# Tile 0's products with the high weights of two panels, done during tile 1's norm at two joints

## The reference

```python
def layer_norm(x, g, b):
    mu = jnp.mean(xf, axis=-1, keepdims=True)
    var = jnp.mean(jnp.square(xf - mu), axis=-1, keepdims=True)
    y = (xf - mu) * lax.rsqrt(var + LN_EPS)
    return y * g + b

def post_norm(x, sub, g, b):
    return layer_norm(DN_ALPHA * x + sub, g, b)

def swiglu(x, w1, w3, w2):
    return (jax.nn.silu(x @ w1) * (x @ w3)) @ w2
```

## Time and profile before

| | us |
|---|---|
| median of 3 runs | 2235.81 (2235.27 to 2235.83) |
| span of the profiled execution, first to last instruction | 2233.5 |
| the profiled execution's own time | not shown; the median is 2.3 above its span |
| TensorE busy | 2197.0 (98%) |
| VectorE busy | 1568.6 (70%) |
| ScalarE busy | 1170.0 (52%) |
| TensorE's granted clock, mean | 0.999 |

### The profile page before, as it was taken

One profiled execution on the slowest core, in us unless ns is written; L12 is line 12 of the kernel. 1 busy time (PEld: TensorE's weight loads), 2 busy tenths in 40 slices (PEclk: granted clock), 3 DMA queues, 4 the chain that ended last, 5 costly groups with the idle time before them and its releaser, 6 DMA issues. The chain is left out here.

```text
span 2233.5 us, 37259 instructions
## 1 busy us (share of the span) xinstructions
PE 2197.0 (98%) x14678; PEld 1964.0 (88%) x14678; DVE 1568.6 (70%) x2935; ACT 1170.0 (52%) x2008; POOL 33.9 (2%) x20
## 2 busy tenths in 40 slices
PE   8999999999999999999999999999999999999998
PEld 8987889999999998888888889988889788888887
DVE  7975659999889976666666557766657465776655
ACT  6643454555554455565555455545544544585544
POOL 0100000010000000000000000000000000000000
PEclk9999999999999999999999999999999999999999
DMA  7418425555444456666655556536455655404552
GB/s 275 151 46 189 170 93 174 181 178 170 144 150 143 150 171 192 194 194 193 194 189 212 190 190 240 191 127 232 176 200 191 248 186 192 175 34 175 184 204 97
DMA packets 78310, 389.98 MB, mean 175 GB/s; under 512 B 9771, under 2 KB 12715, under 8 KB 49868
## 3 DMA queue, kind: packets, MB, share of 16 engines
q1 hardware_dynamic: 76684, 383.33, 49.3%
q0 software_dynamic: 1040, 4.19, 1.5%
q10 hardware_dynamic: 432, 0.33, 0.0%
HBM read 382.57 MB, written 5.24 MB: 174 GB/s over the span
## 5 line engine op out<-in xcount | busy, mean ns | idle before, releaser
L256 DVE TENSOR_TENSOR split_slots<-ring,split_slots 128x1024 fp32r<-128x1024 f32 x402 | 475.3, 1227 | 118.4 <-ACT split_slots L247 118.2
L247 ACT ACTIVATE split_slots<-ring 128x1024 fp32r<-128x1024 f32 x402 | 402.3, 1054 | 149.3 <-PE banks L400 123.3
L3107 PE MATMUL banks<-x_transposed,split_slots 128*128 128x512 f32 x1360 | 478.4, 395 | 0.3 <-PEq L464 0.3
L409 DVE SCALAR_TENSOR_TENSOR expert_lo<-ring,expert_hi 128x512 fp32r<-128x512 f32 x512 | 353.4, 697 | 165.7 <-ACT expert_hi L404 164.6
L404 ACT ACTIVATE expert_hi<-ring 128x512 fp32r<-128x512 f32 x512 | 324.0, 634 | 252.5 <-PE banks L400 252.5
L3108 PE MATMUL banks<-x_transposed,split_slots 128*128 128x256 f32 x1360 | 381.5, 281 | 0.0
L3107 PEld LDWEIGHTS banks<-x_transposed,split_slots 128*128 128x128 f32 x1360 | 255.3, 188 | 60.4 <-issue 0.5
L398 PE MATMUL banks<-x_transposed,expert_hi 128*128 128x256 f32 x1024 | 293.9, 287 | 2.5 <-DVE expert_lo L409 2.5
L399 PE MATMUL banks<-x_transposed,expert_hi 128*128 128x256 f32 x1024 | 287.8, 281 | 0.0
L400 PE MATMUL banks<-x_transposed,expert_lo 128*128 128x256 f32 x1024 | 287.7, 281 | 0.0
L3108 PEld LDWEIGHTS banks<-x_transposed,split_slots 128*128 128x128 f32 x1360 | 256.4, 189 | 1.5
(11 more groups left out here) (491 smaller groups left out, 4020.5 us busy)
## 6 DMA issues: line engine op xcount, KB each, us to landing
ring<-in_ffn_w SPq DMA_DIRECT2D x132, 1024.0 KB, 4.8
ring<-in_peer_u SPq DMA_DIRECT2D x128, 512.0 KB, 3.5
ring<-in_peer_v SPq DMA_DIRECT2D x128, 512.0 KB, 3.6
ring<-in_w_in SPq DMA_DIRECT2D x16, 1024.0 KB, 6.0
ring<-in_sgu_w_in SPq DMA_DIRECT2D x16, 1024.0 KB, 4.8
ring<-in_peer_wq SPq DMA_DIRECT2D x8, 1024.0 KB, 7.3
ring<-in_sgu_w_out SPq DMA_DIRECT2D x8, 1024.0 KB, 4.9
ring<-in_kv_w SPq DMA_DIRECT2D x6, 1024.0 KB, 4.8
```

The source lines that it names most:

```text
L247: act.activation(self.parts[:, b, 0, p], self.k.w.slot(g)[:, p], ACT.Copy).then_inc(self.high_done, 1)
L256: ins = dve.tensor_tensor(self.parts[:, b, 1, p], self.k.w.slot(g)[:, p], self.parts[:, b, 0, p].bitcast(F32), ALU.subtract)
L409: return dve.scalar_tensor_tensor(dst, src, scale, hi.bitcast(F32), ALU.mult, ALU.subtract)
L3107: pe.matmul(out(j, slice(0, 2 * SEQ)), lh, k.xT.both[:, c, :, :], start=(c == 0), stop=False)
```

## The change

`SecondHigh` lets ScalarE write the high parts of the next stage's second panel during the norm. `TileAhead` then gives TensorE, between the transposes of tile 0 and those of tile 1, the products of both panels' high weights with tile 0: 16 per panel, each with the high and the low part of 128 rows as one operand (two runs of 128 columns), written to two runs of 128 columns of the output bank. The sums are started by products with a tile of zeros that clear the whole bank (`clear`). Behind the joint each panel then has 16 products of its low weights (256 columns) and 16 of the high weights with tile 1 (256 columns). It replaces the stand-ins at norms 1 and 4.

For that VectorE's order is changed. In all six norms: tile 1's first half is added ahead of tile 0's normalising. At norms 1 and 4 also: tile 0's two low parts are written behind tile 1's centring, ahead of its normalising. The first unit's sums lie in banks 0, 1 and 4, 5, the second's in 6, 7 and 4, 5. The diff, cut:

```diff
@@ -225,6 +225,8 @@
         self.beginning = k.beginning
+        self.second = k.second if self.begun else None
+        self.highs_begun = 2 if self.second else self.begun
         self.before = k.before
@@ -234,7 +236,7 @@
     def high(self, act, n, i=0, per=0):
-        if n < self.begun:
+        if n < self.highs_begun:
             return
@@ -252,7 +254,11 @@
             p = slice(half * SLOT // 2, (half + 1) * SLOT // 2)
-            dve.wait_ge(self.high_done, 2 * (n - self.begun) + half + 1 + 2 * per * i)
+            if n < self.highs_begun:
+                if self.before:
+                    dve.wait_ge(self.second.high_done, half + 1)
+            else:
+                dve.wait_ge(self.high_done, 2 * (n - self.highs_begun) + half + 1 + 2 * per * i)
             ins = dve.tensor_tensor(self.parts[:, b, 1, p], self.k.w.slot(g)[:, p], self.parts[:, b, 0, p].bitcast(F32),
...
@@ -309,10 +315,82 @@
+class SecondHigh:
+    def __init__(self, k, first):
+        self.k, self.g = k, first.g + 1
+        self.b = self.g % BUFFERS
+        self.high_done = k.sig.new()
+        k.second = self
+    def highs(self, act):
+        k = self.k
+        act.wait_ge(k.w.loaded[self.g % RING], 16 * (self.g // RING + 1))
+        for half in range(2):
+            p = slice(half * SLOT // 2, (half + 1) * SLOT // 2)
+            act.activation(k.split_parts[:, self.b, 0, p], k.w.slot(self.g)[:, p], ACT.Copy).then_inc(self.high_done, 1)
+class TileAhead:
+    def __init__(self, k, first, second):
+        self.k, self.first, self.second = k, first, second
+    def product(self, pe, begun, bank, j, c, i):
+        k = self.k
+        wh = k.split_parts[:, begun.b, 0, :].rearrange("p (c n) -> p c n", c=DC)
+        own = slice(i * P, (i + 1) * P)
+        out = k.psum[:, bank + j, :].rearrange("p (q n) -> p q n", q=2)[:, :, own]
+        return pe.matmul(out, wh[:, c, j * P:(j + 1) * P], k.xT.both[:, c, :, own], start=False,
+                         stop=(i == 1 and c == DC - 1))
+    def clear(self, pe, bank):
+        k = self.k
+        for j in range(2):
+            pe.matmul(k.psum[:, bank + j, :], k.zero[:, :], k.split_parts[:, self.first.b, 0, 0:2 * SEQ], start=True, stop=False)
+    def tile_0(self, pe, written):
+        g = self.first.g
+        pe.wait_ge(self.k.w.used[g % RING], g // RING + 1)
+        self.clear(pe, 0)
+        for part in range(2):
+            pe.wait_ge(written, part + 1)
+            for j in range(2):
+                for c in range(part * DC // 2, (part + 1) * DC // 2):
+                    self.product(pe, self.first, 0, j, c, 0)
+        pe.wait_ge(self.second.high_done, 2)
+        self.clear(pe, 4)
+        for j in range(2):
+            for c in range(DC):
+                self.product(pe, self.second, 4, j, c, 0)
+    def low_weights(self, pe, begun, bank, chunks):
+        k = self.k
+        wl = k.split_parts[:, begun.b, 1, :].rearrange("p (c n) -> p c n", c=DC)
+        for j in range(2):
+            for c in chunks:
+                pe.matmul(k.psum[:, bank + j, 0:SEQ], wl[:, c, j * P:(j + 1) * P], k.xT.hi[:, c, :], start=False, stop=False)
+    def tile_1(self, pe, begun, bank):
+        for j in range(2):
+            for c in range(DC):
+                ins = self.product(pe, begun, bank, j, c, 1)
+        return ins
 class Before:
...
-    def __init__(self, splits_eaten, highed=None, written=None, banks_read=(), parts=None, turn=None, ahead=0):
+    def __init__(self, splits_eaten, highed=None, written=None, banks_read=(), parts=None, turn=None, ahead=0,
+                 begun=None):
+        self.begun = begun
         self.splits_eaten, self.highed, self.written, self.banks_read = splits_eaten, highed, written, banks_read
...
@@ -431,6 +510,7 @@
         self.eps = self.sb(ctx, "epsilons", [P, 2])
+        self.zero = self.sb(ctx, "zeros", [P, P], F32R)
         self.final_stat = self.sb(ctx, "final_stats", [P, 4, TILES])
@@ -599,6 +679,8 @@
         act.activation(warm[:, :], k.eps[:, 0:1], ACT.Sqrt)
+        act.wait_ge(begun.ident_landed, 16)
+        act.activation(k.zero[:, :], k.ident[:, :], ACT.Copy, scale=0.0)
         for i in range(TILES):
@@ -2686,7 +2768,8 @@
-    def __init__(self, k, ctx, split, gains, which, slots, final=False, squares=None, last=False):
+    def __init__(self, k, ctx, split, gains, which, slots, final=False, squares=None, last=False,
+                 two_ahead=False):
         self.last = last
...
@@ -2726,26 +2810,25 @@
         dve.wait_ge(self.gains_landed, 32)
-        for i in range(TILES):
-            x = k.x[:, i, :]
-            sums = [stat[:, 6 * n, i:i + 1] for n in range(2)]
-            mean = stat[:, 1, i:i + 1]
-            def add(n):
-                own = x[:, self.halves[n]]
-                dve.wait_ge(self.tile_done, 2 * i + n + 1)
-                dve.scalar_tensor_tensor(own, own, DN_ALPHA, k.psum[:, 2 * i + n, :], ALU.mult, ALU.add, accum_out=sums[n]
-                                         ).then_inc(self.summed, 1)
-            add(0)
-            dve.wait_ge(self.summed, 2 * i + 1)
-            dve.tensor_scalar(mean, sums[0], -1.0 / D, None, ALU.mult).then_inc(self.negated, 1)
-            add(1)
-            dve.wait_ge(self.summed, 2 * i + 2)
-            dve.wait_ge(self.negated, 2 * i + 1)
-            dve.scalar_tensor_tensor(mean, sums[1], -1.0 / D, mean, ALU.mult, ALU.add).then_inc(self.negated, 1)
+        def add(i, n):
+            own, mean = k.x[:, i, self.halves[n]], stat[:, 1, i:i + 1]
+            dve.wait_ge(self.tile_done, 2 * i + n + 1)
+            dve.scalar_tensor_tensor(own, own, DN_ALPHA, k.psum[:, 2 * i + n, :], ALU.mult, ALU.add,
+                                     accum_out=stat[:, 6 * n, i:i + 1]).then_inc(self.summed, 1)
+            dve.wait_ge(self.summed, 2 * i + n + 1)
+            if n == 0:
+                dve.tensor_scalar(mean, stat[:, 0, i:i + 1], -1.0 / D, None, ALU.mult).then_inc(self.negated, 1)
+            else:
+                dve.wait_ge(self.negated, 2 * i + 1)
+                dve.scalar_tensor_tensor(mean, stat[:, 6, i:i + 1], -1.0 / D, mean, ALU.mult, ALU.add).then_inc(self.negated, 1)
+        def centre(i):
             dve.wait_ge(self.negated, 2 * i + 2)
-            dve.scalar_tensor_tensor(accumulated(k, i), x, stat[:, 1, i:i + 1], gains[:, 0, :], ALU.add, ALU.mult
+            dve.scalar_tensor_tensor(accumulated(k, i), k.x[:, i, :], stat[:, 1, i:i + 1], gains[:, 0, :], ALU.add, ALU.mult
                                      ).then_inc(self.gained, 1)
+        def normalise(i):
             dve.wait_ge(self.rooted, i + 1)
@@ -2753,8 +2836,19 @@
                                          ALU.mult, ALU.add).then_inc(self.normed, 1)
+        add(0, 0)
+        add(0, 1)
+        centre(0)
+        add(1, 0)
+        normalise(0)
+        add(1, 1)
+        centre(1)
+        if self.ahead:
+            self.low(dve, 0)
+            self.low(dve, 1)
+        normalise(1)
         if self.begin:
-            for b in range(4):
+            for b in range(2 if self.ahead else 0, 4):
                 self.low(dve, b)
@@ -2765,6 +2859,9 @@
             if self.begin and i == 1:
+                if self.ahead:
+                    self.split.finished(act, self.free + 1)
+                    self.ahead.second.highs(act)
                 self.high(act, 0)
@@ -2780,8 +2877,9 @@
         self.k.before = Before((self.tile_done, 2 * TILES), (self.highed, 4), (self.written, 4), ((self.written, 1),),
-                               turn=self.turn_last)
+                               turn=self.turn_last, begun=self.ahead)
         self.k.gains_free = self.normed
+        self.k.ahead = self.ahead
@@ -2790,17 +2888,19 @@
             stand_in(pe, self.k, 3)
-            if self.which != 0:
+            if self.ahead:
+                self.ahead.tile_0(pe, self.written)
+            elif self.which != 0:
                 pe.wait_ge(self.negated, 2 * TILES)
...
                 self.turn_last(pe, range(DC))
-                stand_in(pe, self.k, 8)
-def last_products(pe, k, tile_done, ready, operands, rows):
+                stand_in(pe, self.k, 8, 3)
+def last_products(pe, k, tile_done, ready, operands, rows, eaten=None):
@@ -2810,7 +2910,8 @@
         for half in range(2):
-            part(0, i, r, half)
+            ins = part(0, i, r, half)
+        return ins
@@ -2824,7 +2925,9 @@
     late(0)
-    early(1, 1)
+    ins = early(1, 1)
+    if eaten:
+        ins.then_inc(eaten, 1)
     late(1)
...
@@ -2876,7 +2979,7 @@
             last_products(pe, k, norm.tile_done, ready, lambda n, r: k.xT.at(slice(0, P), 2 * (last + n) + r),
-                          lambda n: split.rows(last + n))
+                          lambda n: split.rows(last + n), split.eaten)
             norm.tensor(pe)
@@ -3058,6 +3161,7 @@
         copied, joined = ([k.sig.new() for _ in range(2)] for _ in range(2))
+        ahead = k.ahead
```

(39 more changed lines are left out.)

## The result

| | median us | lowest to highest | runs |
|---|---|---|---|
| kernel before | 2235.82 | 2235.01 to 2237.80 | 20 |
| changed kernel | 2238.76 | 2237.53 to 2241.58 | 20 |

The account below looks back on a forecast made before the run. TensorE, busy for 98% of the span, was taken as the bound. Late joint 0.0, early joint 0.0, stall 0.2 and norms 2.1 summed to +2.3 us: span 2235.8, time 2238.1, range 2233 to 2242.

Parts of the forecast that it names:

- Late joint: Joint at about 2036 us: 3.8 us saved behind tile 1's transposes, 3.8 lost ahead of them, net 0.0.
- T: Start of tile 1's transposes on TensorE, 2041.03 us at the late joint, 1500.44 at the early; forecast 3.8 later at each.
- Early joint: Joint at about 1500 us, followed by a barrier: 3.8 us saved, tile 1's transposes 3.8 later, net 0.0.
- stall of 0.2: Early joint, fourth panel: TensorE may wait for VectorE's join of the second panel's sums; 0.2 us, bounds nothing and 1.0.
- sign of being wrong: At the fourth panel, a wait of over 0.5 us would show the prediction wrong.
- the near end: Fourth panel's wait: 0.2 us taken between bounds of nothing and 1.0, near the end that the sum itself gives.
- Plain norms: Three other norms that begin a next panel: VectorE's new order makes each 0.63 us late, together 1.9.
- the last norm: Norm without high parts on ScalarE: only the shift of the mean stays, 0.24 us.
- The 2.3 added to the span: Difference between the median, 2235.81 us, and the profiled span, 2233.5, carried over to the forecast time.
- Hidden: Rival, both joints: tile 0's products end before tile 1 is ready, transposes +1.0 instead of +3.8, time 2232.5 us; 10%.
- Clock: Rival, hole before tile 1's transposes: clock falls to 1.2 GHz, work there about 3.4 us longer per joint, 2244.9 us; 7%.
- Split output: Rival, tile products writing two runs of 128 columns take 0.234 us each, not 0.119; time 2253 us; 6%.

Follow-up runs that it names:

- e3: Changed kernel with the fourth panel's transfer issued ahead of the gains' and biases' transfers at both joints; 2237.66 us, ratio 1.0007 to the kernel before.
- e8: Kernel before with 14 stand-ins in place of 8 ahead of the barrier at 1164 us; 2236.23 us, ratio 0.9998 to the kernel before.
- e1: Changed kernel with VectorE's old order in the four norms that do nothing ahead; 2236.87 us, ratio 1.0003 to the kernel before.
- e6: Changed kernel with 8 more stand-ins at each joint, between tile 0's products and tile 1's transposes; 2242.87 us, ratio 1.0029 to the kernel before.
- e9: e7 with the second panel's products with tile 0 moved behind tile 1's transposes at the early joint, replacing 8 stand-ins; 2232.28 us, ratio 0.9981.
- e7: e5 with 14 stand-ins in place of 8 ahead of the barrier at 1164 us; 2232.79 us, ratio 0.9983 to the kernel before.
- e4: Changed kernel with tile 0 normalised before adding tile 1, and its low parts written before tile 1's centring, at both joints; 2235.95 us, ratio 0.9999.
- e5: Changed kernel with VectorE's old order in all norms, tile 0's low parts before tile 1's centring, fourth panel's transfer before the gains; 2232.76 us, ratio 0.9983.

## Why the prediction was right, and the term that was off

- **Late joint, 0.0.** Measured: T +3.78 from the last product (said 3.8), the part behind T -3.85 (said -3.8). The first low part let TensorE start at 2044.99, 4.28 behind the last product; VectorE's queue, worked out, gave 2040.46 - 2036.18 = 4.28.
- **Early joint, 0.0 and a stall of 0.2.** The joint itself measured -0.2: T +3.79, but 0.3 less from T to the barrier, which the prediction had called unchanged. The stall came by the path that was named (landing, split, silu, copy, join); its size was the term that failed: 1.07 where 0.2 was taken, above the upper bound of 1.0 and above the 0.5 that the prediction itself named as a sign of being wrong. e3, which only moves that one issue, takes away 1.1, and the wait with it. The prediction took the near end because with the old landing the join had 0.2 us to spare. That landing was one reading of 8.0; the one of this profile is 9.35, 1.35 later, and everything behind it in ScalarE's queue with it, less the 0.3 to spare. Why it is 9.4 in one profile and 8.0 in another stays open: e8 has 9.4 without the sooner transfer.
- **Plain norms, 3 x 0.63.** Measured 0.58, 0.62 and 0.61; the last norm 0.2 (said 0.24). e1 returns 1.9 of the 2.1.
- **The sum.** With 1.07 for 0.2 it is +3.2. The trace's own terms are -0.1 (late), -0.2 and 1.07 (early), 1.8 and 0.2: +2.8, and the medians say +2.9. So the forecast of +2.3 is near by its mechanism, and a little by luck: the 0.9 that the stall was short of was met by 0.3 that the joints gave and nobody forecast. The rest of the 3.1 between the spans, 0.2, lies between the norms at 1692 and 1935 and isn't of the change: e8, the kernel before with 6 more stand-ins, has it too (243.21 between these last products, before 242.95).
- **The 2.3 added to the span** was 2.0 to 2.1 in all runs on record; it stands on both sides and doesn't touch the difference.
- ***Hidden* (10%)** is denied: the late one in front of T is TensorE, and e6's 1.78 us of added work came out in full. e9 shows the point from which it would hold, one panel less, in that kernel's order on VectorE.
- ***Clock* (7%)** is denied in the place it named. The changed kernel's stretches across the hole, two at the late joint and one at the early (columns as in the earlier trace rows):

```profile
2041.00:2043.00 2.00, 1.49 (x12) 1.14 (x12) 1.97 (x5) 0.97 (x3) 0.00 (x0) 1.00 0.00 0
2043.00:2045.00 2.00, 1.08 (x9) 0.64 (x7) 1.96 (x4) 1.97 (x4) 0.00 (x0) 1.00 0.03 8
1501.00:1503.00 2.00, 1.07 (x9) 1.04 (x9) 1.89 (x5) 0.95 (x3) 0.00 (x0) 1.00 0.00 0
```

  The figure behind the five engines' brackets, 1.00, is the granted clock; it is 1.00 too in the stretches between and behind, up to 2047 and 1507. The holes of 0.51 and 0.92 us (early joint: 0.56 and 0.93) left it at its higher level. The 3.4 us that this rival was priced at are worked out from no row; what a fall costs is read in the last section.
- ***Split output* (6%)** is denied: 16 products with two runs of 128 columns start 0.12 us apart (2047.45 to 2049.34, so 1.89 / 16 = 0.118), and the 16 with low weights, whose output is one run, as well (2054.51 to 2056.41, so 1.90 / 16). The Trainium skill, "SBUF — State Buffer", section "Door 1: The DMA port swizzle", says that any access to PSUM that isn't contiguous slows matmuls significantly. The trace doesn't agree for runs of this length.

## What to carry to other kernels

Work moved into a hole of the bounding engine counts only as far as the hole lasts beyond the moment its operand is ready: here one panel fitted with 0.7 us of delay to T and the second put T off by another 1.6 of its 2.4 (e9 against e7), and writing the operand ahead of tile 1's centring (e4) brought T 1.5 to 1.6 us sooner at each joint. An order changed for one place is paid for wherever the same function is called: here in four norms that got nothing for it, 1.9 us. And where a stage gets shorter by moving work ahead, look for what hangs on the landing of a transfer: a join that was just in time becomes the wait. One trace gives one landing; over the profiles here the same transfer landed 8.0 to 9.5 us after the barrier, so to take 0.2 from one reading was too fine.

## What the hardware showed beyond this

TensorE's clock can fall behind a hole at which, in other executions, it stays. Behind the barrier at 1164 us, profiled execution of the changed kernel: TensorE's row behind the hole, and then the stretches (length, busy and count of PE, PEld, DVE, ACT, POOL, granted clock, DMA, GB/s); they answer to the earlier trace rows:

```profile
1166.50 1.94 PE L655 MATMUL banks<-ident,x_natural 128*128 128x128 f32 x8 [2.02 <-PEq L559]
```

```profile
1166.00:1168.00 2.00, 1.50 (x7) 1.53 (x8) 1.47 (x3) 0.38 (x1) 0.00 (x0) 0.63 0.24 63
1168.00:1170.00 2.00, 2.00 (x11) 1.77 (x10) 1.38 (x2) 1.65 (x3) 0.00 (x0) 0.52 1.00 277
1170.00:1172.00 2.00, 2.00 (x19) 2.00 (x19) 1.74 (x2) 2.00 (x3) 0.00 (x0) 1.00 1.07 442
```

TensorE idled 2.02 us, and behind it the clock is at the lower of its levels, 1.2 of 2.4 GHz, until 1170: 11 products in two microseconds instead of 20. In the profile of before the hole was 1.56 and the clock stayed at 1.00. The length of the hole doesn't decide alone: in e3's profile it was 1.56 too and the clock fell to 0.55, in e6's it was 2.26 and the clock stayed. It fell in 3 of the 8 profiles with 8 stand-ins at this barrier (changed kernel, e3, e5). From the row behind the hole to the last product ahead of the norm at 1350 it takes 185.07, 185.42 and 185.06 us in these three, and 183.88 or 183.89 in all eight others: a fall costs 1.2 to 1.5 us.

It also fits the tail of the runs: with 8 stand-ins, 12 of 82 runs of the changed kernel and e1 to e6 are over 1.3 us above their own median, and 16 of 77 runs of the kernel before in the experiments' batches. The three profiled executions whose clock fell are 1.4, 2.1 and 1.9 above their medians, and the mean granted clock over the whole run is 0.998 in 20 of these 28 long runs, and in 1 of the 164 others (all batches together); the rest have 0.999. With 14 stand-ins (e7, e8, e9) no run of 33 is that long, and the hole is 0.30, 0.30 and 1.06; e7's row and stretches:

```profile
1166.45 1.07 PE L655 MATMUL banks<-ident,x_natural 128*128 128x128 f32 x8 [0.30 <-PEq L559]
```

```profile
1166.00:1168.00 2.00, 1.45 (x12) 1.09 (x11) 1.59 (x4) 0.88 (x2) 0.00 (x0) 1.00 0.30 100
1168.00:1170.00 2.00, 2.00 (x19) 2.00 (x18) 1.64 (x3) 1.91 (x3) 0.00 (x0) 1.00 0.92 242
```

The median is no better for it. That every long run is such a fall is argued from this, not shown: a run without a profile doesn't say where its clock was low. Why some executions fall and others don't with the same hole stays open.
